# A gated delta scan that sums its squares step by step, straight from the output banks

## The reference

```
def step(S, xs):
    u_c, w_c, qd_c, att_c, kt_c, gt_c = xs
    v_new = u_c - w_c @ S                       # per head
    o_c = qd_c @ S + att_c @ v_new
    S = S * gt_c + kt_c^T @ v_new
    return S, o_c
...
o = rms_norm(o, norm_w) * silu(z)               # rms over the 128 features of a head
return o.reshape(B, L, GDN_VAL_DIM) @ w_out
```

## Time and profile before

| what | value |
|---|---|
| median of three runs | 1448.69 us |
| profiled execution, time | 1448.88 us |
| its span in the trace | 1447.0 us |
| TensorE busy | 1426.9 us, 99% |
| VectorE, ScalarE, GpSimd busy | 1013.5, 778.9, 293.7 us |
| granted TensorE clock in the scan | 1.00 |
| scan in the trace, first prior to first gdn_out matmul | 216.14 to 265.79 us |

### The profile page before, as it was taken

The page is one execution under the profiler, slowest core; times in us unless marked ns, Lnnn a source line. Parts: engine busy times, 40 slices in busy tenths (PEclk is TensorE's granted clock), DMA queues, the critical chain, the costliest instruction groups (busy, mean ns, idle before and its releaser), DMA issues.

```text
span 1447.0 us, 31771 instructions
## 1 busy us (share of the span) xinstructions
PE 1426.9 (99%) x11333; PEld 1366.7 (94%) x11333; DVE 1013.5 (70%) x1701; ACT 778.9 (54%) x1399; POOL 293.7 (20%) x348
## 2 busy tenths in 40 slices
PE   9999999999999999999999999999999999999997
PEld 8999888899999999999999999999999989999986
DVE  7884957659876476569888477587664687776645
ACT  6556324456655366456665356465453567654542
POOL 3804002103544000002444000013330012033310
PEclk9999999999999999999999999999999999999999
DMA  6551221244655535343666644546556433465652
GB/s 255 178 175 46 88 89 59 86 148 147 194 178 177 175 112 187 112 135 127 190 192 186 188 130 160 162 141 198 185 174 196 154 120 118 159 219 185 182 182 91
DMA packets 60996, 223.57 MB, mean 155 GB/s; under 512 B 6768, under 2 KB 6896, under 8 KB 60528
## 3 DMA queue, kind: packets, MB, share of 16 engines
q1 hardware_dynamic: 60624, 220.17, 47.9%
q10 hardware_dynamic: 288, 2.23, 0.4%
HBM read 221.32 MB, written 1.05 MB: 154 GB/s over the span
## 4 chain that ended last, share of the span: by engine, by line
PE 80%; DVE 12%; ACT 4%; issue 3%; DVEq 1%; ACTq 0%; POOL 0%; POOLq 0%
PE bank L440 20%; PE bank L441 20%; PE bank L442 20%; DVE wlo L415 3%; PE bank L461 2%; PE bank L1168 2%; PE bank L462 1%; PE bank L468 1%; DVE bank L947 1%; PE bank L3283 1%; PE bank L3284 1%; PE bank L3286 1%; ACT cv L831 1%; DVE cv L839 1%; DVE work L1782 1%
## 5 line engine op out<-in xcount | busy, mean ns | idle before, releaser
L415 DVE TENSOR_TENSOR wlo<-raw,whi 128x1024 fp32r<-128x1024 f32 x397 | 501.5, 1268 | 249.5 <-ACT whi L410 248.9
L410 ACT ACTIVATE whi<-raw 128x1024 fp32r<-128x1024 f32 x397 | 415.1, 1056 | 290.1 <-PE bank L442 242.0
L440 PE MATMUL bank<-xs,whi 128*128 128x258 f32 (+2 forms) x1984 | 569.3, 287 | 1.1 <-DVE wlo L415 1.1
L441 PE MATMUL bank<-xs,whi 128*128 128x258 f32 (+2 forms) x1984 | 563.9, 284 | 0.0
L442 PE MATMUL bank<-xs,wlo 128*128 128x258 f32 (+2 forms) x1984 | 561.6, 283 | 0.0
L440 PEld LDWEIGHTS bank<-xs,whi 128*128 128x128 f32 x1984 | 374.3, 189 | 4.4 <-DVE wlo L415 1.7
L442 PEld LDWEIGHTS bank<-xs,wlo 128*128 128x128 f32 x1984 | 375.0, 189 | 0.0
L441 PEld LDWEIGHTS bank<-xs,whi 128*128 128x128 f32 x1984 | 374.3, 189 | 0.6 <-issue 0.2
L440 PE MATMUL bank<-hf,whi 128*128 (+3 forms) x848 | 241.3, 285 | 1.9 <-DVE cv L839 0.8
L441 PE MATMUL bank<-hf,whi 128*128 (+3 forms) x848 | 240.3, 283 | 0.0
L442 PE MATMUL bank<-hf,wlo 128*128 (+3 forms) x848 | 240.3, 283 | 0.0
(11 more groups left out here) (516 smaller groups left out, 1679.4 us busy)
## 6 DMA issues: line engine op xcount, KB each, us to landing
raw<-stream SPq DMA_DIRECT2D x412, 512.0 KB, 3.6
con<-consts SPq DMA_DIRECT2D x1, 1284.5 KB, 10.4
big<-mla ACTq DMA_DIRECT2D x1, 1152.0 KB, 8.1
hs_sb<-hs SPq DMA_DIRECT2D x2, 544.0 KB, 4.3
work<-last ACTq DMA_DIRECT2D x1, 1024.0 KB, 8.6
y_out<-work SPq DMA_DIRECT2D x4, 256.0 KB, 2.0
par<-params SPq DMA_DIRECT2D x1, 420.0 KB, 7.8
par<-params SPq DMA_DIRECT2D x1, 224.0 KB, 4.8
```

The costliest lines, as they stand in the source:

```text
L410: nc.scalar.activation(whi[:, s, :], raw[:, s, :], ACT.Copy).then_inc(hi_split, 1)
L415: nc.vector.tensor_tensor(wlo[:, s, :], raw[:, s, :], whi[:, s, :].bitcast(F32), ALU.subtract).then_inc(block_split, 1)
L440: nc.tensor.matmul(out_, whi[:, slot, w], hi, start=start, stop=False)
L441: nc.tensor.matmul(out_, whi[:, slot, w], lo, start=False, stop=False)
```

## The change

- TensorE's state update writes into columns 256 to 511 of the same bank as the outputs (bank 4 or 5), so that bank 6 is free from the start of the scan.
- The squares are summed per step: `step_squares(n-3)` at the end of every iteration from 3 on, two matmuls of 144 columns (c=1: the 16 of the head chunk and 128) or 128 columns (c=2), into bank 6. The strip of 48 columns stays. The last is a call behind the loop.
- ScalarE squares straight from the output bank, both heads in one instruction (and for c=1 the 16 head columns from SBUF), after VectorE has read the bank. TensorE's outputs two steps on wait for both readers.
- VectorE multiplies the outputs with the gate where it copied them; for c=1 it now waits for the state update too. GpSimd's 16 products go; one over the 16 head columns of all heads remains. Gates are made six or more steps earlier, partly before the scan.
- Row matmuls move to bank 7, row 0 to iteration 13, row 1 to the end of iteration 14. ScalarE issues two of its high parts between the last squares, and the fourth after `row_scale(1)`.

```diff
--- before.py
+++ after.py
@@ -1055,7 +1055,11 @@
-    o_sq = [wk(4096 + T1 * i, T1) for i in range(7)]
+    SQ_SLOTS = 6
+    bank_read = lambda n: f"S{n}" if ORDER[n][1] == 1 else f"o{n}"
+    o_sq = [wk(4096 + 288 * i, 288).rearrange("p (a t) -> p a t", a=2) for i in range(SQ_SLOTS)]
+    sq_cols = lambda c: slice(0, HEAD_T + P) if c == 1 else slice(HEAD_T, HEAD_T + P)
+    sum_cols = lambda c: slice(0, HEAD_T + P) if c == 1 else slice(HEAD_T + P, T1)
...
@@ -1454,7 +1458,8 @@
         def outputs(n):
             k, c = ORDER[n]
             if n > 1:
-                pe.wait_ge(*v.at(f"o{n - 2}"))
+                pe.wait_ge(*v.at(bank_read(n - 2)))
+                pe.wait_ge(*a_.at(f"sq{n - 2}"))
...
             last.then_inc(*m.mark(f"o{n}"))
             if c == 1:
                 pe.wait_ge(*v.at(f"vd{n}"))
-                if n:
-                    pe.wait_ge(*v.at(f"S{n - 1 if n != 8 else 3}"))
-                mm(bank[6][:, 0:256], ktok(k, 1), vd_buf[n % 2][:, :], start=True, stop=True).then_inc(*m.mark(f"s{n}"))
-
-        def squares(g, heads):
-            for h in heads:
-                pe.wait_ge(*a_.at(f"sq{h}"))
-                last = mm(bank[7][0:GROWS, 0:T1], strip(h), o_sq[h % 7], start=False, stop=(h % 8 == 7))
-                last.then_inc(*m.mark(f"ss{h}"))
-
-        def first_square(g):
-            if g:
+                mm(bank[4 + n % 2][:, 256:512], ktok(k, 1), vd_buf[n % 2][:, :], start=True, stop=True).then_inc(*m.mark(f"s{n}"))
...
+        def step_squares(n):
+            k, c = ORDER[n]
+            if n == 8:
                 pe.wait_ge(*a_.at("ln0"))
-            else:
-                pe.wait_ge(*v.at("qd11"))
-            mm(bank[7][0:GROWS, 0:T1], cn("qsum"), ssq_all, start=True, stop=False)
+            if n % 8 == 0:
+                mm(bank[6][0:GROWS, 0:T1], cn("qsum"), ssq_all, start=True, stop=False)
+            pe.wait_ge(*a_.at(f"sq{n}"))
+            for a in range(2):
+                last = mm(bank[6][0:GROWS, sum_cols(c)], strip(2 * k + a), o_sq[n % SQ_SLOTS][:, a, sq_cols(c)], start=False, stop=(n % 8 == 7 and a == 1))
+            last.then_inc(*m.mark(f"ss{n}"))
...
@@ -1496,26 +1497,20 @@
                 values(n - 1)
             if n >= 2:
                 outputs(n - 2)
-            if n == 12:
-                first_square(0)
-                squares(0, range(0, 6))
-            if n == 13:
-                squares(0, range(6, 8))
-            if n == 15:
-                first_square(1)
+            if n >= 3:
+                step_squares(n - 3)
             for h in ROWS_LAST.get(n, ()):
                 row(h)
-            if n >= 16:
-                squares(1, range(8 + 4 * (n - 16), 12 + 4 * (n - 16)))
-
-    ROWS_FIRST, ROWS_LAST = {15: (1,), 16: (3,), 17: (5, 6)}, {14: (0,), 15: (2,), 16: (4,), 17: (7,)}
+        step_squares(NSTEP - 1)
+
+    ROWS_FIRST, ROWS_LAST = {16: (3,), 17: (5, 6)}, {13: (0,), 14: (1,), 15: (2,), 16: (4,), 17: (7,)}
...
+    row_bank = lambda h: ROW_BANK.get(h, 7)
...
-        read = {0: v.at("S11"), 5: v.at("d14"), 6: v.at("d15"), 8: a_.at("ln1")}
+        read = {0: v.at("qd11"), 5: v.at("d14"), 6: v.at("d15")}
...
-        pe.wait_ge(*{2: a_.at("v14"), 3: a_.at("v15"), 4: v.at("o14"), 5: v.at("o15"), 6: v.at("f7"), 7: v.at("f14"),
+        pe.wait_ge(*{2: a_.at("v14"), 3: a_.at("v15"), 4: v.at("o14"), 5: v.at("o15"), 6: a_.at("ln1"), 7: v.at("f14"),
...
@@ -1656,26 +1651,37 @@
         z_out_act(act, 12)
         below64(1)
         above64(0)
+        for h in (2, 3):
+            silu(h)
         z_out_act(act, 13)
         above64(1)
-        for j in range(14, 16):
-            z_out_act(act, j)
+        for h in (4, 5):
+            silu(h)
+        z_out_act(act, 14)
+        for h in (6, 7):
+            silu(h)
+        z_out_act(act, 15)
...
-            A(o_row, bank[7][0:GROWS, 0:T1], ACT.Ln, scale=1.0 / GD, bias=con_eps[0:GROWS, 1:2]).then_inc(*a_.mark(f"ln{g}"))
+            A(o_row, bank[6][0:GROWS, 0:T1], ACT.Ln, scale=1.0 / GD, bias=con_eps[0:GROWS, 1:2]).then_inc(*a_.mark(f"ln{g}"))
...
+        def square(n):
+            k, c = ORDER[n]
+            t = o_sq[n % SQ_SLOTS]
+            if n >= SQ_SLOTS:
+                act.wait_ge(*m.at(f"ss{n - SQ_SLOTS}"))
+            if c == 1:
+                A(t[:, :, 0:HEAD_T], big[:, 16 + 2 * k:18 + 2 * k, 0:HEAD_T], ACT.Square).then_inc(*a_.mark(f"sq_head{n}"))
+            act.wait_ge(*v.at(bank_read(n)))
+            A(t[:, :, HEAD_T:HEAD_T + P], pairs_of(bank[4 + n % 2][:, 0:256], P), ACT.Square).then_inc(*a_.mark(f"sq{n}"))
...
-            if n + 1 < 16 and n <= 10:
-                silu(n + 1)
-            if n == 10:
-                for h in range(12, 16):
-                    silu(h)
+            if n >= 17:
+                gdn_hi(act, n - 17)
+            if n >= 3:
+                square(n - 3)
+            if n <= 8:
+                silu(n + 7)
             if n in (4, 6, 8):
                 split_hi(act, FIRST_BLOCK["gdn_out"] + n // 2 - 2)
+            if n == 9:
+                nc.scalar.preload_act_table_set(LN_EXP)
             if n == 11:
-                nc.scalar.preload_act_table_set(LN_EXP)
-            if n >= 3 and ORDER[n - 3][1] == 2:
-                k = ORDER[n - 3][0]
-                act.wait_ge(*v.at(f"o{n - 3}"))
-                for h in (2 * k, 2 * k + 1):
-                    if h != 7:
-                        square(h)
-            if n == 13:
-                square(7)
                 row_scale(0)
-        for k in range(4):
-            gdn_hi(act, k)
+        gdn_hi(act, 2)
         row_scale(1)
+        gdn_hi(act, 3)
...
-                dve.wait_ge(*m.at(f"o{n - 2}"))
-                nc.vector.tensor_copy(big[:, 16 + 2 * k:18 + 2 * k, CHUNKS[c][0]:CHUNKS[c][0] + P],
-                                      pairs_of(bank[4 + n % 2][:, 0:256], P)).then_inc(*v.mark(f"o{n - 2}"))
+                dve.wait_ge(*m.at(f"s{n - 2}" if c == 1 else f"o{n - 2}"))
+                dve.wait_ge(*a_.at(f"silu{2 * k + 1}"))
+                x = big[:, 32 + 2 * k:34 + 2 * k, CHUNKS[c][0]:CHUNKS[c][0] + P]
+                tt(x, pairs_of(bank[4 + n % 2][:, 0:256], P), x, ALU.mult).then_inc(*v.mark(f"o{n - 2}"))
                 if c == 1:
                     dve.wait_ge(*m.at(f"s{n - 2}"))
                     for a in range(2):
                         h = 2 * k + a
-                        stt(state[:, h, :], state[:, h, :], col(gt, 1, h), bank[6][:, a * P:(a + 1) * P],
+                        stt(state[:, h, :], state[:, h, :], col(gt, 1, h), bank[4 + n % 2][:, 256 + a * P:384 + a * P],
...
-        dve.wait_ge(*S("gdn", "pool").at(f"x{h}"))
+        dve.wait_ge(*S("gdn", "pool").at("x_head"))
+        dve.wait_ge(*S("gdn", "dve").at(f"o{ORDER.index((h // 2, 2))}"))
...
-        for n in range(NSTEP):
-            k, c = ORDER[n]
-            if c == 2:
-                for h in (2 * k, 2 * k + 1):
-                    pool.wait_ge(*a_.at(f"silu{h}"))
-                    pool.wait_ge(*a_.at("o0"))
-                    pool.wait_ge(*v.at(f"o{n}"))
-                    tt(big[:, 32 + h, :], big[:, 32 + h, :], big[:, 16 + h, :], ALU.mult).then_inc(*pl.mark(f"x{h}"))
+        pool.wait_ge(*a_.at("silu15"))
+        pool.wait_ge(*a_.at("o0"))
+        tt(big[:, 32:48, 0:HEAD_T], big[:, 32:48, 0:HEAD_T], big[:, 16:32, 0:HEAD_T], ALU.mult).then_inc(*pl.mark("x_head"))
```

More of the change, by code:

```diff
@@ L1498, in gdn_pe @@
                 outputs(n - 2)
-            if n == 12:
-                first_square(0)
-                squares(0, range(0, 6))
-            if n == 13:
-                squares(0, range(6, 8))
-            if n == 15:
-                first_square(1)
+            if n >= 3:
+                step_squares(n - 3)
             for h in ROWS_LAST.get(n, ()):
                 row(h)
-            if n >= 16:
-                squares(1, range(8 + 4 * (n - 16), 12 + 4 * (n - 16)))
-    ROWS_FIRST, ROWS_LAST = {15: (1,), 16: (3,), 17: (5, 6)}, {14: (0,), 15: (2,), 16: (4,), 17: (7,)}
+        step_squares(NSTEP - 1)
+    ROWS_FIRST, ROWS_LAST = {16: (3,), 17: (5, 6)}, {13: (0,), 14: (1,), 15: (2,), 16: (4,), 17: (7,)}
     ROW_BANK = {5: 0, 6: 1, **{h: (7, 0, 1)[(h - 8) % 3] for h in range(8, 16)}}
-    row_bank = lambda h: ROW_BANK.get(h, 6)
+    row_bank = lambda h: ROW_BANK.get(h, 7)
     def gdn_row_pe(pe, h):
@@ L1673, in row_scale @@
             A(ro, o_row, ACT.Copy).then_inc(*a_.mark(f"ro{g}"))
-        def square(h):
-            if h > 6:
-                act.wait_ge(*m.at(f"ss{h - 7}"))
-            A(o_sq[h % 7], big[:, 16 + h, :], ACT.Square).then_inc(*a_.mark(f"sq{h}"))
+        def square(n):
[7 more added lines that the diff above has]
+            A(t[:, :, HEAD_T:HEAD_T + P], pairs_of(bank[4 + n % 2][:, 0:256], P), ACT.Square).then_inc(*a_.mark(f"sq{n}"))
         for n in range(1, NSTEP + 3):
```

## The result

| kernel | median us | runs | lowest to highest | ratio to before |
|---|---|---|---|---|
| before | 1446.90 | 20 | 1446.31 to 1449.86 | |
| after | 1449.35 | 20 | 1448.84 to 1452.02 | 1.0016 [1.0010, 1.0022] |

A forecast was written before the change was run, and what follows sets the result against it. TensorE, busy 1426.9 of 1447.0 us, was taken as the bound; 0.1 + 3.4 - 1.5 + 0.3 + 0 + 0.1 + 0.4 = plus 2.8 us on 1448.88 gave 1451.7, forecast as 1451.5 us, own range 1449.5 to 1453.5, wider range 1447.0 to 1455.0.

The forecast's parts named there:

- Columns, plus 0.1: The squares' matmuls on TensorE: same columns in more, shorter instructions, 7.5 us for 7.4, so plus 0.1 us.
- switches, plus 3.4: TensorE in the scan: eleven more bursts switching between 128 and 48 stationary columns, 0.31 us each there and back.
- The rival of free switches: Switching stationary width on TensorE costs nothing, so the kernel is not slower: 1447.5 us, chance 0.22.
- that row: Profile row for fp32r squares of the same strip width: the next 128-column weights load 0.12 us ahead, without a break.
- the other end of one price: Lower end for the price of a width switch on TensorE: zero, against the 0.31 us taken.
- VectorE's waits, minus 1.5: TensorE's waits for VectorE in iterations 7, 9 and 11 go: 0.48 + 0.59 + 0.41 us.
- Squares late, plus 0.3: TensorE waits 0 to 0.2 us for ScalarE's squares at eight places; plus 0.3 in all, ends 0 and 1.6.
- become the bound: Rival: ScalarE becomes the bound, each square 0.3 us late on 14 steps: 1455.4 us, chance 0.15.
- Rows, nothing: Row matmuls in the scan: row 0 waits 0.7 us, row 1 saves 0.65, row 3 keeps 0.69; together nothing.
- End of the scan, plus 0.1: After the last iterations TensorE waits 0.1 us for step 15's square; gdn_out waits for low part 0 as before.
- row 8, plus 0.4: Behind the scan, row matmul 8 waits for the second row scale, delayed by high and low parts: plus 0.4 us.
- the mark that I named: Sign that the forecast is right: gdn_out's first matmul starts 2.3 us later than 265.79.

The follow-up runs named there:

- The padding: Strip for squares and epsilon term padded with zeros from 48 to 128 columns: in the changed kernel 1446.88 us, in the kernel before 1445.46 us.
- the pairs: Changed kernel with the squares of two steps issued together, 9 bursts instead of 16, strip still 48 columns: 1447.85 us, 1.0004 of before.
- (8): Changed kernel with the 128-column strip, plus each step's square ahead of the copy of the values on ScalarE: 1445.19 us, 0.9987 of before.
- the combined kernel: Changed kernel with 128-column strip, squares ahead of ScalarE's value copy, earlier rows and scale, and fourth low part later: 1442.15 us, 0.9967 of before.
- the other two edits: Each alone on the changed kernel: VectorE's fourth low part behind its second row scale share, 1450.29 us; rows 0 to 3 and first scale earlier, 1447.28 us.

## Why the prediction was right, and where it was not

The sum was plus 2.8 us, and plus 2.71 on the path is what came, 2.8 in the times without the drop. Step by step:

- **Columns, plus 0.1, and switches, plus 3.4.** Iteration 4 rose by 0.81, which is four instructions of 144 columns at 0.125 and 0.31. The padding took 0.32 or 0.33 back where nothing else waited, the pairs 0.32 to 0.38 a switch: eleven are 3.5 to 3.6. The rival of free switches is out for fp32. That rival rested on the fp32r row, and that row told the truth about fp32r: what I called the other end of one price was the price of another data type. The Trainium skill, "TensorEngine Tiling (Array Packing)", Key Properties, has the drain at a change of tiling mode as a rule; the fp32 bursts follow it at 0.32 us, the fp32r bursts of the same shape do not. That the break in the loads is such a drain is not shown; the runs show the break, its price, and that it goes with the width.
- **VectorE's waits, minus 1.5.** They are gone: iterations 7 and 9 took 2.53 and 2.77 for 2.5 and 2.8 forecast, and the product 0.42. That value was right, but not its reason, that from 128 to 256 columns an operation grows by less than a tenth: in before's trace a copy from a bank takes 292 ns with 128 columns (L3020) and 418 with 256 (L1852). The row that gives the value is in the same trace, outside the scan: products of 128x256 with a bank operand at 422 ns (L947). Iteration 11 took 3.72 for 3.2: I had forgotten there that the second epsilon matmul (0.5 us) moves into it. It left iteration 15, so the sum did not change.
- **Squares late, plus 0.3.** Iterations 6 to 9 came out at 2.63, 2.53, 2.77 and 2.77 us, where columns and switch alone make 2.58, 2.52, 2.76 and 2.76: 0.1 of lateness at four of the eight places, 0.2 less than the whole term. ScalarE did not become the bound. Its head square took 0.22 for 0.2. Its squares were late all the same, and the switch covered that: with the padding it came out (8).
- **Rows, nothing.** Row 0 waits 0.87 for 0.7 and row 1 no longer. By the starts that is 0.94 more and 1.25 - 0.44 = 0.81 less (row 1 started 1.25 after a prior that takes 0.44): plus 0.1.
- **End of the scan, plus 0.1, and row 8, plus 0.4.** The last square waits 0.18, but gdn_out's first matmul 0.17 for 0.41: about nothing. Row 8 comes 0.63 later.
- **The total.** So measured, the terms are 0.1 + 3.5 - 1.5 + 0.1 + 0.1 + 0 + 0.6 = 2.9 for 2.71; the 0.2 left over I did not trace. Most terms were off by 0.1 or 0.2 in either direction and cancelled. The mechanism was right, and that the sum met the path within 0.1 was luck.
- **The base was wrong.** I put the sum on 1448.88 and took it for 0.2 above the median. It was an execution with the clock drop; the undisturbed base is 1446.4, and the sum on it gives 1449.2. So 1451.5 was 2.1 too high with every term in place: 1449.35 is inside the range of 1447.0 to 1455.0, and just below the forecast's own, 1449.5 to 1453.5. The three times shown (1449.16, 1448.69, 1446.31) held the hint: two together and one 2.4 lower is no spread of one quantity. The windows of the whole span, which I had not read outside the scan, held the proof. It also upset the mark that I named, a first gdn_out matmul 2.3 us after 265.79: it came at 265.62, yet 2.08 later counted from the first prior.

## What to carry to other kernels

Try a narrow fp32 stationary operand padded to 128 columns, or fp32r where its rounding may be had, before asking where its matmuls should stand; only then does a spread over the steps cost no switches, and only then do the squares' producer and the row chain decide. When a stall is taken away, ask engine by engine what TensorE now reaches too soon: here 2.9 us came at once, and 4.7 with the orders of ScalarE and VectorE changed as well (7.20 on the path of the combined kernel, less the 0.64 and 1.85 of the other two edits). And read the granted clock over the whole span before using one profiled execution as a base.

## What the runs showed of the hardware

- **An early clock drop in a part of the executions.** In the twelve profiled executions the mean granted clock between 116 and 126 us was 1.00 five times (first prior at 213.57 to 213.95), 0.83 twice (214.35 and 214.51) and 0.66 five times (216.04 to 216.29), whatever the kernel. TensorE did the same ahead of it in both kinds: 1.43 and 1.44 of 2.00 us busy from 116 to 118, at a clock of 1.00. Why it falls in one and not in the other, the traces do not tell; no run was made for it.
- **The price of a narrow fp32 operand** is 0.32 us there and back at a granted clock of 1.00, for strips of 48 columns; an fp32r strip of that width gains nothing from 128 columns (2.39 us with 48, 2.43 with 128). No other width was tried.
- **A product on VectorE of a bank and an SBUF operand**, 128x256 fp32, takes 424 ns, about as long as the copy from the bank, 418.
